# Value projections as split products of 256 columns, and split tiles for the memory's keys, in a two-block transformer kernel

## What is computed

```python
h = rms_norm(x, norm_mix[l])
proj = h @ w_in[l]
q, k, v, u = jnp.split(proj, [ATTN_WIDTH, 2 * ATTN_WIDTH, 3 * ATTN_WIDTH], axis=-1)
...
xn = rms_norm_2(h, norm_mix[l])
z = xn @ w_in[l]
z_r, z_q, z_kc, z_vc, z_ks, z_vs, z_kw, z_vw, z_g, z_m = jnp.split(z, split_pts, axis=-1)
...
h = h + merged.astype(h.dtype) @ w_mix_out[l]
...
def cross_attn(xn, mn, wq, wkv, q_gain, k_gain, wo):
    q = rms_norm_2((xn @ wq).reshape(B, S, CA_HEADS, CA_HEAD_DIM), q_gain, QK_EPS)
    kv = (mn @ wkv).reshape(B, M, 2, CA_HEADS, CA_HEAD_DIM)
    k = rms_norm_2(kv[:, :, 0], k_gain, QK_EPS)
    v = kv[:, :, 1]
    s = jnp.einsum('bshd,bmhd->bhsm', q, k).astype(jnp.float32) * (CA_HEAD_DIM ** -0.5)
    p = jax.nn.softmax(s, axis=-1).astype(v.dtype)
    o = jnp.einsum('bhsm,bmhd->bshd', p, v).reshape(B, S, CA_HEADS * CA_HEAD_DIM)
    return o @ wo
```

## Time and profile before

| | |
|---|---|
| median of 3 executions | 2137.32 us (2131.4 to 2138.85) |
| the profiled execution | 2136.98 us, of which 2134.8 us is the profile's span |
| PE busy | 2081.1 us (97%), 15222 records |
| DVE busy | 1094.6 us (51%) |
| ACT busy | 787.2 us (37%) |
| POOL busy | 323.3 us (15%) |
| conversions of weights | 251 on ACT at 1047 ns, 251 on DVE at 1234 ns |
| weight transfers | 276 of 512 KB, 3.5 us each to landing |

### The profile page before, as it was taken

How to read it: one execution, slowest core, us unless ns; L and a number is a source line. 1 busy time by engine, 2 the same in 40 slices (tenths; PEclk the granted TensorE clock), 3 DMA queues, 4 the chain that set the end, 5 groups by cost and what they waited for, 6 DMA issues and landing times.

```text
span 2134.8 us, 35749 instructions
## 1 busy us (share of the span) xinstructions
PE 2081.1 (97%) x15222; PEld 1631.0 (76%) x15222; DVE 1094.6 (51%) x1794; ACT 787.2 (37%) x1343; POOL 323.3 (15%) x396
## 2 busy tenths in 40 slices
PE   8989999999999999998999999989999999999999
PEld 6847888888766699995778785558787877888887
DVE  5255444444657644446535745553554346666432
ACT  4164333232555422224323526664234243232211
POOL 0451000000304400002200026641230020000000
PEclk9999999999999999999999989999999999999999
DMA  5203232232242210000347220013232132322322
GB/s 181 65 30 99 90 98 90 98 99 89 95 154 79 64 39 4 4 4 23 109 133 250 73 86 1 1 70 99 89 99 89 60 109 89 99 89 94 96 92 84
DMA packets 47518, 177.05 MB, mean 83 GB/s; under 512 B 5328, under 2 KB 5840, under 8 KB 46593
## 3 DMA queue, kind: packets, MB, share of 16 engines
q1 hardware_dynamic: 43488, 154.12, 22.2%
...
## 4 chain that ended last, share of the span: by engine, by line
PE 92%; DVE 4%; ACT 2%; issue 1%; POOL 0%; DMA 0%; SPq 0%; DVEq 0%; ACTq 0%; POOLq 0%
PE ps L301 22%; PE ps L302 21%; PE ps L306 21%; PE ps L2468 8%; PE ps L808 3%; PE ps L1314 2%; PE ps L2481 2%; PE ps L1298 1%; PE ps L1567 1%; PE ps L2893 1%; ACT arena L1409 1%; PE ps L1267 1%; DVE arena L1370 1%; DVE arena L1354 1%; PE ps L1722 1%
## 5 line engine op out<-in xcount | busy, mean ns | idle before, releaser
L281 ACT ACTIVATE w_hi<-wring 128x1024 fp32r<-128x1024 f32 (+1 forms) x251 | 262.8, 1047 | 566.2 <-PE ps L306 559.8
L287 DVE TENSOR_TENSOR w_lo<-wring,w_hi 128x1024 fp32r<-128x1024 f32 (+1 forms) x251 | 309.6, 1234 | 249.5 <-ACT w_hi L281 248.1
L301 PE MATMUL ps<-ffn_input_hi,w_hi 128*128 128x512 f32 x352 | 139.5, 396 | 0.0
L302 PE MATMUL ps<-ffn_input_hi,w_lo 128*128 128x512 f32 x352 | 139.1, 395 | 0.0
L2468 PE MATMUL ps<-arena 64*64 64x64 f32 x3776 | 126.9, 218 | 3.6 <-issue 2.2
L2468 PEld LDWEIGHTS ps<-arena 64*64 64x64 f32 x3776 | 122.1, 135 | 10.6 <-issue 8.2
L1456 POOL TENSOR_TENSOR arena<-arena 128x512 f32<-128x512 f32 (+3 forms) x160 | 111.4, 721 | 39.2 <-DVE arena L1362 34.2
L2568 ACT ACTIVATE arena<-ps 128x512 f32<-128x512 f32 x94 | 56.1, 597 | 162.1 <-PE ps L2468 162.1
L301 PE MATMUL ps<-gate_input_hi,w_hi 128*128 128x512 f32 x256 | 106.0, 414 | 1.5 <-ACT gate_input_hi L853 1.5
L301 PE MATMUL ps<-mlp_input_hi,w_hi 128*128 128x512 f32 x256 | 101.6, 397 | 0.0
L301 PE MATMUL ps<-mlp_hi,w_hi 128*128 128x512 f32 x256 | 101.2, 395 | 0.0
...
## 6 DMA issues: line engine op xcount, KB each, us to landing
wring<-weights SPq DMA_DIRECT2D x276, 512.0 KB, 3.5
...
```

What stands on the lines that cost most here:

```text
L281: act.activation(self.w_hi[:, m % SPLIT, 0:n], self.wring[:, g % RING, 0:n], ACT.Copy).then_inc(self.w_hi_ready, 1)
L287: dve.tensor_tensor(self.w_lo[:, m % SPLIT, 0:n], self.wring[:, g % RING, 0:n], self.w_hi[:, m % SPLIT, 0:n].bitcast(F32), ALU.subtract).t ...
L301: pe.matmul(out, hi[:, c, :], src.hi[:, at + c, :], start=(at + c == 0), stop=False)
L302: pe.matmul(out, lo[:, c, :], src.hi[:, at + c, :], start=False, stop=False)
```

## The change

- `pv` and `pvs` become `SplitTokens`: the weights of 256 outputs stand in two units (`token_units`), the stationary operand is the hi or lo part of the input that the projections before them read already, and 256 columns of hi or lo weights move. `Normalized` and its f32 tiles go. Since the split input of the first block carries no root, `RootTokens` transposes the root to one value per token, and the drain scales by it.
- The compressed softmax (`vector_step`, `scalar_step`) runs inside the loop of `pvs`. The last two units of `pvs` do their lo x hi products first and then release the low part of the input (`lo_used`), in whose place the copied keys go; `Spread` waits for that and makes 8 copies of twice the size, 4 for the first heads.
- `nm` starts one unit earlier in `bn`. `ms2` writes the normed memory as hi and lo parts beside `pm`.
- The keys become a `SplitProjectNorm` on 256 columns with the mean of `nx` inside it, the values split units that are converted between the steps of the cross attention and drained in pairs.

```diff
-class Normalized(Stage):
...
-    def tile_vector(self, dve, j):
-        dve.scalar_tensor_tensor(self.dst[:, j, :], self.src[:, j, :], self.k.vec(self.gain, j), self.root,
-                                 ALU.mult, ALU.mult).then_inc(self.k.xn_ready, 1)
...
+class SplitTokens(SplitStage):
...
+    def __init__(self, k, src, drains, after, lo_used=None):
+        super().__init__(k, after)
+        self.src, self.drains = src, drains
+        self.lo_used = k.sem(lo_used) if lo_used else None
+        self.root_tokens = self.beside = None
+        for _ in drains:
+            pair = [k.take_acc(), k.take_acc()]
+            self.ts.append(pair)
+            self.us += [[k.take_split(pair[1], UNIT, last=(half == 1))] for half in range(2)]
...
+    def product(self, pe, i, b, c, kind, start=False, stop=False):
+        k, src, unit = self.k, self.src, self.us[i][0]
+        w = (k.w_lo if kind == "hi lo" else k.w_hi)[:, unit % SPLIT, :].rearrange("p (c m) -> p c m", m=self.WIDE)
+        x = (src.lo if kind == "lo hi" else src.hi)[:, self.HALF * (i % 2) + c, b * P:(b + 1) * P]
+        out = k.acc(self.ts[i // 2][b // 2])[:, (b % 2) * self.WIDE:(b % 2 + 1) * self.WIDE]
+        return pe.matmul(out, x, w[:, c, :], start=start, stop=stop)
...
+    def unit(self, pe, i, low):
+        k, half = self.k, i % 2
+        self.wait_weights(pe, i, True)
+        kinds = ("hi hi", "hi lo", "lo hi") if low else ("hi hi", "hi lo")
+        for n, t in enumerate(self.ts[i // 2]):
+            if half == 0 and low:
+                k.open_acc(pe, t)
+            for b in (2 * n, 2 * n + 1):
+                for c in range(self.HALF):
+                    for kind in kinds:
+                        mm = self.product(pe, i, b, c, kind, start=(low and half == 0 and b % 2 == 0 and c == 0 and kind == "hi hi"),
+                                          stop=(half == 1 and b % 2 == 1 and c == self.HALF - 1 and kind == kinds[-1]))
+            if half == 1:
+                mm.then_inc(k.acc_full, 1)
+        if half == 0:
+            mm.then_inc(k.split_used, 1)
+    def tensor(self, pe):
+        k = self.k
...
+        last = len(self.us) - 2 if self.lo_used is not None else len(self.us)
+        for i in range(last):
+            self.unit(pe, i, True)
+        if self.lo_used is None:
+            return
+        for i in (last, last + 1):
+            self.wait_weights(pe, i, False)
+            for b in range(NT):
+                if i == last and b % 2 == 0:
+                    k.open_acc(pe, self.ts[i // 2][b // 2])
+                for c in range(self.HALF):
+                    mm = self.product(pe, i, b, c, "lo hi", start=(i == last and b % 2 == 0 and c == 0))
+        mm.then_inc(self.lo_used, 1)
+        self.unit(pe, last, False)
+        self.unit(pe, last + 1, False)
...
+    def scalar(self, act):
+        self.convert_first(act, self.k.convert_hi)
+        for i in range(len(self.us)):
+            self.convert_next(act, self.k.convert_hi, i)
+            if self.beside is not None:
+                self.beside.scalar_step(act, i)
+            for n in range(2 if i % 2 else 0):
+                self.drains[i // 2](act, self.ts[i // 2][n], n)
...
+        for i in range(len(self.us)):
+            if self.beside is not None:
+                self.beside.vector_step(dve, i)
+            self.convert_next(dve, self.k.convert_lo, i)
...
+class RootTokens:
...
+    def tensor(self, pe):
+        k = self.k
...
+        for b in range(NT):
+            mm = pe.transpose(k.aux(self.t)[:, b * P:(b + 1) * P], k.root[:, b * P:(b + 1) * P], k.const("ident"))
+        mm.then_inc(k.aux_full, 1)
+    def vector(self, dve):
+        k = self.k
+        k.wait_aux_full(dve, self.t)
+        dve.tensor_copy(self.dst, k.aux(self.t)[:, 0:3 * P + 1:P]).then_inc(k.aux_drained[self.t % NX], 1)
...
+        root.wait(act)
+        for b in range(2):
+            at = 2 * n + b
+            ins = act.activation(dst[:, at, :], src[:, b, :], ACT.Copy, scale=root.dst[:, at:at + 1])
...
+    def vector_step(self, dve, i):
...
+        if i == 1:
+            self.shift(dve, x, m)
+        if i == 2:
+            self.scale(dve, x, m)
...
+    def scalar_step(self, act, i):
+        if i == 1:
+            act.wait_ge(self.shifted, 1)
+            x = row(self.table)
+            act.activation(x, x, ACT.Exp).then_inc(self.p_ready, 1)
...
+                k.split_product(pe, k.acc(self.ts[i])[:, 0:self.n], self.us[i], self.src, wait=(i == 0))
+                if i == 0 and self.norm is not None:
+                    self.norm.mean(pe)
...
+                if i == 0 and self.norm is not None:
+                    act.wait_ge(k.square_used, self.norm.used0 + DT_ - 1)
...
+            if i == self.outs and self.filler is not None:
+                self.filler.low(dve, 1)
...
-            for g in range(NKV):
-                self.waits[b](pool, g // 2)
-                e = g % 2
+        self.wait(pool)
+        for e in range(2):
+            for b in range(2):
                 for half in range(2):
-                    pool.dma_start(self.dst[b][half * HD:(half + 1) * HD, g, :],
-                                   self.src[b][e * HD:(e + 1) * HD, g // 2, :]).then_inc(self.done, 16)
...
+    WIDE, HALF = 256, 4
...
+        hi, lo = (w[:, unit % SPLIT, :].rearrange("p (c m) -> p c m", m=self.WIDE) for w in (k.w_hi, k.w_lo))
         for b in range(N_MEM // P):
-            for c in range(DT_):
-                mm = pe.matmul(k.acc(t)[:, b * P:(b + 1) * P], self.src[:, c, b * P:(b + 1) * P], w[:, c, :],
-                               start=(c == 0), stop=(c == DT_ - 1))
...
     def vector(self, dve):
+        self.tiles.low(dve, 2)
         for h in range(4):
             self.maxima(dve, h)
             self.scale(dve, h)
...
+        self.tiles.high(act, 2)
         self.exps(act, 0)
-        self.tiles.copy(act, 1)
+        self.tiles.copy(act, 0)
...
-            for i in self.BEHIND_TURNS[h]:
-                self.tiles.copy(act, i)
-                if i == 6:
-                    self.begin.convert(act)
+            if h == 0:
+                self.tiles.high(act, 4)
+            if h == 1:
+                self.tiles.copy(act, 1)
+                self.tiles.high(act, 5)
+            if h == 2:
+                self.tiles.high(act, 6)
...
-        pv = Project(k, 4, tiles(xn32), nv.wait_dst,
-                     [copy_tokens(k, v1[:, :, i * P:(i + 1) * P], P) for i in range(4)], kind="tokens")
+        roots = RootTokens(k, view(38800, [NT]), lambda pe: k.wait_acc_drained(pe, pq.ts[0]))
+        pv = SplitTokens(k, n1, [wide_tokens(k, v1[:, :, i * 256:(i + 1) * 256], roots) for i in range(2)], after=pu)
+        pv.root_tokens = roots
...
-        spread = Spread(k, kraw, kd, [lambda e, g, b=b: (k.wait_acc_full(e, nq.ts[-1]), nq.wait_dst(e, DT_ + 2 * b + g)) for b in range(2)])
-        pvs = [Project(k, 2, tiles(xn), lambda pe, c: None,
-                       [copy_tokens(k, vs[b][:, :, i * P:(i + 1) * P], P) for i in range(2)], kind="tokens")
-               for b in range(2)]
+        pvs = SplitTokens(k, xs6, [wide_tokens(k, vs[b]) for b in range(2)], after=nq, lo_used="gate_input_lo_used")
+        pvs.beside = cs
+        spread = Spread(k, kraw, kd, lambda e: (pvs.wait_lo_used(e), nq.wait_dst(e, DT_ + 3)))
...
-        nm = NormBeside(k, bn, mem_t, mem_t, "norm_mem", lambda e, j: load_mem.wait_done(e), N_MEM, first=DT_)
+        nm = NormBeside(k, bn, mem_t, mem_t, "norm_mem", lambda e, j: load_mem.wait_done(e), N_MEM, first=DT_ - 1)
...
+        pm.beside = ms2
         nx = Norm(k, k.x, xn32, "norm_cross", drained(pm), source=pm, apart=True)
...
-        pk = ProjectNorm(k, 8, tiles(mem_t), nm.wait_dst, tiles(k3), tiles(k3),
-                         lambda i: k.vec("ca_k_gain", i % 2), "ones256", span=2, n=N_MEM, beside=nx)
+        v3, o3 = view(18432, [2, D]), view(4096, [DT_, S])
+        pk = SplitProjectNorm(k, 8, ms2, tiles(k3), tiles(k3), lambda i: k.vec("ca_k_gain", i % 2), "ones256", span=2, n=N_MEM,
+                              norm=nx, after=pm)
         xs8 = HostedTiles(k, pk, "cross_input", xn32, view_r("cross_input_hi", 28672, [DT_, S]),
                           view_r("cross_input_lo", 20480, [DT_, S]), nx.wait_dst)
-        begin_cross = Begin(k, pk, inside=True)
-        mv = MemoryValues(k, mem_t, v3)
+        mv = MemoryValues(k, None, v3)
         pq3 = SplitProjectNorm(k, 8, xs8, tiles(q3), tiles(q3), lambda i: k.vec("ca_q_gain", i % 2), "ones256", span=2,
-                               after=begin_cross, filler=mv)
+                               after=pk, filler=mv)
+        mv.src = ms2
...
+def token_units(w):
+    wide = [w[:, i:i + 256].reshape(2, 4, P, 256).transpose(0, 2, 1, 3).reshape(2, P, 1024) for i in range(0, w.shape[1], 256)]
+    return [half for pair in wide for half in pair]
...
```

187 lines of the change are left out of this document (123 added, 64 removed).

## The result

The changed kernel takes 2142.64 us (median of 10, 2138.12 to 2146.73) against 2136.69 for the kernel before (median of 10): a ratio of 1.0036, 95% interval 1.0026 to 1.0047. I had said 2136.6. So the change costs 6 us by the medians and 7.7 (5.6 to 10.0) by the ratio, inside the range I gave, but clear of zero, where I had forecast none. The profiled execution took 2142.57 us, of which 2140.7 is its span; before it was 2136.98 and 2134.8.

What follows compares the result with a forecast made beforehand. TensorE (PE), busy 97% of the span, was taken as the bound. Terms -5.2, -5.6, -3.5, +12.3, +2.2 and -0.6 summed to -0.4 us, giving 2136.6 from 2136.98: no change, range 2127 to 2151.

Steps and rivals of the forecast that it cites:

- Part 1: First block's value projection: 192 split products and four transposes replace 128 plain products; -5.2 us (-7 to -4).
- Part 2: Second block's two value projections: product work falls from 28.8 to 23.0 us; -5.6 us in sum (-7.5 to -2).
- (b): Key copies wait for the input's low parts, yet land before attention with 1 to 2 us margin; 0 to 3 if not.
- 1 MB takes some 6.3 us: Key copies before the second block's attention: landing time taken from the earlier trace's first eight issues (4.16 us, landing in 2.2 to 4.1).
- Part 3: Border of gated and mix projections: starting the memory's norm one step earlier cuts PE's waits; -3.5 us (-4.5 to -2).
- The refinement meets no POOL work: End of the gated projection: one step earlier, DVE's refinement for the memory's norm runs without POOL busy; no separate size.
- The sentence on the memory's hi and lo parts: Beside the mix projection: 8 ACT and 8 POOL operations hide behind 5.6 us per mix unit, costing nothing.
- Part 4: Memory's keys: DVE's conversion behind eight cross-norm tiles idles PE about 12 us; +12.3 (+8 to +15), plus +2.2 for the clock.
- The first rival: Memory's keys: clock stays at half speed to the stage's end, pitch 0.127; +29 there, total 2155 us; chance 0.13.
- Part 5: Memory's values and cross attention: 5.5 us less PE work, mostly lost to DVE and copy waits; -0.6 us (-2 to +1).

Runs made afterwards that it cites:

- e3_spread: The changed kernel, with POOL waiting until the first four key copies have landed before issuing the other four; 2144.32 us, 1.0049 of the kernel before.
- e8_pool: The changed kernel, with POOL starting its mix low parts only after DVE's eight products of the memory's norm; 2144.57 us, 1.0039 of the kernel before.
- e5_first8: The changed kernel, with the memory's norm begun in the same gated-projection unit as in the kernel before; 2143.27 us, 1.0041 of the kernel before.

## Why the prediction was off by 6 us

- **Part 1**, right: -4.9 for -5.2, with 3.4 us at 1.2 GHz in it (from 112.4); the four kernels without such a stretch here show -5.7. Pitch 0.118 for 0.120.
- **Part 2**, the price right and (b) mis-sized: -4.1 for -5.6. The work went by 28.8 - 22.7 = 6.1. But PE waited 3.46 for the copies, where I had a margin of 1 to 2 us and gave its failure 0 to 3. The step that failed is "1 MB takes some 6.3 us", read from eight issues of half the size with the shortest time to landing, 2.2. The eighth of them took the longest, 4.1, and had landed 7.7 us after the first issue; and the four copies of 256 KB took 10.0 here, 9.5 alone in e3_spread. The release of the low parts was at 1245.2, 7.2 us ahead of the last product, which I had at 7.7.
- **Part 3**, wrong in sign: +2.8 for -3.5, and the largest miss; this is the step on which the forecast of no change failed. I carried the eight products over at 3.25 us, the duration of the earlier trace rows, into a place where POOL works beside them; the same rows had shown what POOL does to a neighbour (a conversion at 2.19 for 1.22), and I used it only for what had been there before. "The refinement meets no POOL work" was true, and its successor met it instead: 7.37 us, and a wait of 4.45 before the mix projection where I had named under 2. e8_pool shows that cause. The sentence on the memory's hi and lo parts, "nothing", failed too: they are new POOL work beside DVE, and with the norm left where it was (e5_first8) the stages cost 2.8 all the same, by the rows for that reason.
- **Part 4**, right in mechanism and size: a hole of 11.66 for 12, released by the conversion on DVE, 48.3 us for 47.2, and the clock low behind it. The first rival, that it stays slow to the end of the stage, didn't come: it rose at 1580.1 and fell once more at 1593.8. Two readings under this part were wrong. Between 1570.17 and 1574.48 has 16 records, so 8 products and not 16; the price of 0.43 is right even so. And the 5.5 us at half speed of the earlier trace rows were the end of a stretch of 13.7; around this hole the clock was low for 10.2 to 13.7 us, where I had taken 3.4 to 5.5.
- **Part 5**: +0.8 for -0.6. The conversion ahead of the first maxima, which I had seen, made a wait of 2.23 us, and the clock fell once more behind it. In the two kernels with the same code in which it didn't fall the part gave -0.9 and -0.7, as forecast.
- **Outside the parts**: -1.6 for an input that landed earlier (the twelve kernels with this start have 7.95 to 9.88 us, and the changed kernel's profile is the lowest), -4.3 and +2.2 for the clock in unchanged code, together -3.7. These were drawn, not earned; without them the profiled difference would be 9.6 us. The profiled executions lie at the medians of their kernels all the same (2142.57 for 2142.64, 2136.98 for 2136.69), so in sum their luck was ordinary. How it was spread in the other executions the runs don't tell.

The parts are drawn in part as well. Over all kernels here that share the changed kernel's code in a part, they spread like this: part 1 -5.7 to -4.0, part 2 -4.8 to -3.0, part 3 +1.4 to +2.8, part 4 +14.6 to +16.8, part 5 -0.9 to +0.8, each against the one profile of before. Part 3 stays wrong in sign in every one of them.

So the total came out within 6 us for mixed reasons. The parts as measured sum to +10.2 where I had -0.4: 6.3 us too low in part 3, 1.5 in part 2, 1.1 to 1.4 in each of parts 4 and 5 and 0.3 in part 1. Against this stand 3.7 of draw and 0.6 in the rest.
